# Expert stage of a three-block network: first two activation chunks as one group of 512 columns, and the expert one-hot written by ScalarE from a table

## The chip, the core and the metric

The kernel runs on one core of one Trainium2 chip. The metric is the device time of one execution in microseconds (us), from the first to the last instruction with what lies around them. Engines are named as in the profile: PE is TensorE (PEld its weight loads), DVE is VectorE, ACT is ScalarE, POOL is GpSimd, SP is SyncE, which issues the weight DMAs.

## The reference, cut to what matters

Three network blocks run one after the other on 512 tokens of width 1024. The change touches the mixture of experts at the end of the first block alone:

```python
def moe(h, w_router, b_router, w1, b1, w2, b2):
    """Top-4-of-32 experts with clamped SwiGLU; exact sparse dispatch via expert-sorted blocks."""
...
x = x + gt_f[:, None, :] * moe(h, w_router[l], b_router[l], w_mlp1[l], b_mlp1[l], w_mlp2[l], b_mlp2[l])
```

For each expert, up to 128 of its tokens are gathered. The first product, 1024 to 2048 columns plus bias `b1`, gives a gate half and a linear half. The activation is the gate, clamped above at 7, times its sigmoid (with 1.702), times the clamped linear half plus one. The second product, 1024 to 1024, is scaled by the token's gate and added to the token's row.

## The kernel before

A unit is one expert with up to 128 tokens. There are 34 units in this run (32 experts and spills). The loop body in each engine's program is one unit; the last unit stands behind the loop. All fp32 products are made from pairs of float32r numbers: a high part (`moe_high`, written by ACT, L1802) and a low part (`moe_low`, written by DVE, L1811). A unit has 24 half chunks j of weights (128x1024 each), 16 for the first product and 8 for the second. `high(j)` is one ACT instruction; `low(j)` is one DVE instruction for the halves j and j+1 together (128x2048). Six halves of buffer stand between them and PE, so `high(j)` waits until PE has used half j-6 (semaphore `used`).

`pe_unit` (L2034) sets PE's order. For each of four activation chunks c it adds the bias by a product of the one-hot `moe_esel` with `b1` (L2061), then four `product` calls of six matmuls (L2050 four, L2054 two). The output is bank 0 or 1 of PSUM, by c modulo 2. Behind chunk 1 comes `turn(0)`, two transposes of the activated chunk 0 (L2041); behind chunk 2 `turn(1)`, behind chunk 3 `turn(2)`. Then come the eight halves 16 to 23 of the second product, with the eight transposes of the next unit's tokens (`pe_x_turn`, L2030, into banks 4 and 5) behind half 17, and `turn(3)` behind half 18. A `turn(c)` waits for `multiply(c)` (`act_done`) and for `low_of_turned(c-1)` (`aT`).

`dve_unit` (L1870) sets DVE's order, by hand: between the `low` instructions stand, for each chunk, `clamp` (L1885, linear half out of PSUM), `multiply` (L1891, then L1894, of 256 columns each) and `low_of_turned` (L1879). `dve_stage` (L1845, L1846) writes the next unit's token indices for the gather. It waits for `kept`: POOL's copy L1948 of the present indices, which stands on POOL behind the scatter L1962 of the unit before. `dve_esel` (L1851) writes the one-hot from a PSUM column. `dve_xe_low` (L1858) writes the low part of the next unit's transposed tokens; PE's next unit waits for it (`xe`). `act_unit` (L1979) has the `sigmoid` (L1988), `turned` (L1993, high part of the transposed activations) and `act_xe` (L1976).

Of the kernel before, what the change touches and what calls it, by code (L numbers as in the profile page):

```python
# [20 lines left out]
ALU = mybir.AluOpType  # L21
# [1750 lines left out]
class Experts:  # L1772


    def __init__(self, K, bufs):
        self.K, self.nc, self.B = K, K.nc, bufs
        n_ = lambda s: K.sem(f"moe_{s}")
        self.used, self.high, self.low = n_("used"), n_("high"), n_("low")
        self.picked, self.placed, self.read, self.staged = n_("picked"), n_("placed"), n_("read"), n_("staged")
        self.esel = n_("esel")  # L1780
# [35 lines left out]

    def split(self, part, eng, u, js, ahead):
# [31 lines left out]
    def dve_esel(self, ve, v):  # L1849
        B = self.B  # L1850
        self.nc.vector.tensor_scalar(B["esel"][:, :], B["ps_row"].to_broadcast([P, CAP]),  # L1851
                                     B["unit_f"][:, bass.ds(v, 1)], None, ALU.is_equal).then_inc(self.esel, 1)

    def dve_xe_low(self, ve, v):
        B = self.B
        ve.wait_ge(self.xe_high, v + 1)
        flat = lambda part: B["xe"][:, part, :, :].rearrange("p k n -> p (k n)")
        self.nc.vector.tensor_tensor(flat(1), self.K.ps[:, 4:6, :].rearrange("p a n -> p (a n)"),  # L1858
                                     flat(0).bitcast(F32), ALU.subtract).then_inc(self.xe, 1)
# [10 lines left out]
    def dve_unit(self, ve, u, ahead=True):  # L1870
        nc, B = self.nc, self.B

        def low(*js):
            self.split(self.dve_low, ve, u, js, ahead)

        def low_of_turned(c):
            ve.wait_ge(self.aT_high, u * 4 + (c + 1))
            out = B["aT"][:, :, 2 * c:2 * c + 2, :]
            nc.vector.tensor_tensor(out[:, 1, :, :].rearrange("p a b -> p (a b)"), self.K.ps[:, 3, 0:256],  # L1879
                                    out[:, 0, :, :].rearrange("p a b -> p (a b)").bitcast(F32), ALU.subtract)\  # L1880
                .then_inc(self.aT, 1)

        def clamp(c):
            ve.wait_ge(self.used, u * PER + (4 * c + 4))
            nc.vector.tensor_scalar(B["lin"][:, c % 2, :], self.K.ps[:, c % 2, 256:512], 1.0 + LIMIT, 1.0 - LIMIT,  # L1885
                                    ALU.min, ALU.max).then_inc(self.clamped, 1)

        def multiply(c):
            ve.wait_ge(self.sig, u * 4 + (c + 1))
            ve.wait_ge(self.clamped, u * 8 + (2 * c + 1))  # L1890
            nc.vector.scalar_tensor_tensor(B["glu"][:, c % 2, :], B["sig"][:, c % 2, :], SIG_LIMIT, B["lin"][:, c % 2, :],  # L1891
                                           ALU.min, ALU.mult).then_inc(self.clamped, 1)
            ve.wait_ge(self.clamped, u * 8 + (2 * c + 2))
            nc.vector.scalar_tensor_tensor(B["a"][:, c % 2, :], self.K.ps[:, c % 2, 0:256], LIMIT, B["glu"][:, c % 2, :],  # L1894
                                           ALU.min, ALU.mult).then_inc(self.act_done, 1)
# [78 lines left out]
    def act_xe(self, sc, v):  # L1974
        sc.wait_ge(self.x_turned, v + 1)
        self.nc.scalar.activation(self.B["xe"][:, 0, :, :].rearrange("p k n -> p (k n)"),  # L1976
                                  self.K.ps[:, 4:6, :].rearrange("p a n -> p (a n)"), ACT.Copy).then_inc(self.xe_high, 1)

    def act_unit(self, sc, u, ahead=True):  # L1979
        nc, B = self.nc, self.B  # L1980

        def high(*js):
            self.split(self.act_high, sc, u, js, ahead)

        def sigmoid(c):
            sc.wait_ge(self.clamped, u * 8 + (2 * c + 1))
            sc.wait_ge(self.act_done, u * 4 + (c + 3))
            nc.scalar.activation(B["sig"][:, c % 2, :], self.K.ps[:, c % 2, 0:256], ACT.Sigmoid, scale=ALPHA)\  # L1988
                .then_inc(self.sig, 1)

        def turned(c):
            sc.wait_ge(self.a_turned, u * 4 + (c + 5))
            nc.scalar.activation(B["aT"][:, 0, 2 * c:2 * c + 2, :].rearrange("p a b -> p (a b)"),  # L1993
                                 self.K.ps[:, 3, 0:256], ACT.Copy).then_inc(self.aT_high, 1)
# [32 lines left out]
    def pe_x_turn(self, pe, v):  # L2027
        pe.wait_ge(self.gathered, v * 16 + 16)
        for k in range(KD):
            ins = self.nc.tensor.transpose(self.K.ps[:, 4 + k // 4, (k % 4) * P:(k % 4 + 1) * P],  # L2030
# [3 lines left out]
    def pe_unit(self, pe, u, ahead=True):  # L2034
        nc, ps, B = self.nc, self.K.ps, self.B

        def turn(c):
            pe.wait_ge(self.act_done, u * 4 + (c + 5))
            pe.wait_ge(self.aT, u * 4 + (c + 4))
            for i in range(2):  # L2040
                ins = nc.tensor.transpose(ps[:, 3, i * P:(i + 1) * P], B["a"][:, c % 2, i * P:(i + 1) * P],  # L2041
                                          self.K.ident[:, :])
            ins.then_inc(self.a_turned, 1)
# [15 lines left out]
        for c in range(4):  # L2059
            pe.wait_ge(self.act_done, u * 4 + (c + 3))  # L2060
            nc.tensor.matmul(ps[:, c % 2, :], B["esel"][:, :], B["b1"][:, c * 512:(c + 1) * 512], start=True, stop=False)  # L2061
            for i in range(4):
                product(ps[:, c % 2, :], B["xe"], 4 * c + i, 2 * i, True)
            if c:
                turn(c - 1)
            if c == 0 and ahead:
                self.pe_place(pe, u + 1)
        for j in range(16, 24):
# [3 lines left out]
            if m == 0:  # L2072
                pe.wait_ge(self.aT, u * 4 + (k + 5))
# [3 lines left out]
            if j == 18:  # L2077
                turn(3)
# [7 lines left out]
def mixture(K, posm, gate, gsplit, units, rows, gates_f):  # L2086
# [8 lines left out]
    with ExitStack() as ctx:  # L2095
        sb = lambda name, shape, dt=F32: K.sb(ctx, f"moe_{name}", shape, dt)
        lane = lambda i: K.hT[:, i, :].rearrange("p (b n) -> p b n", b=2)
        iota, from_end, slots = sb("iota", [P, CAP]), sb("from_end", [P, NT]), sb("slots", [P, 8])
# [4 lines left out]
             "ps_row": table[:, 384:385], "ps_place": table[:, 388:392], "from_end": from_end[:, :],  # L2103
# [16 lines left out]
        pair = lambda t: K.ps[:, 6 * ((t + 1) % 2):6 * ((t + 1) % 2) + 2, :]  # L2120
        with nc.Block() as block:
# [41 lines left out]
            def _(ve):  # L2163
# [5 lines left out]
                nc.vector.tensor_copy(B["ps_row"], slots[:, 5:6])  # L2169
# [4 lines left out]
                ve.nop().then_inc(X.act_done, 4)  # L2174
                ve.nop().then_inc(X.aT, 4)
                ve.nop().then_inc(X.y_ready, 2)
                X.dve_esel(ve, 0)
# [36 lines left out]
            def _(sc):  # L2214
# [11 lines left out]
                X.act_xe(sc, 0)  # L2226
                with sc.Fori(0, n1) as u:
# [5 lines left out]
            def _(pe):  # L2233
                n1 = pe.value_load(unit_last[0:1, 0:1], min_val=EXPERTS - 1, max_val=EXPERTS + SPILLS - 1)
                pe.nop().then_inc(X.a_turned, 4)
# [1845 lines left out]
```

## Time and profile before

| | |
|---|---|
| median of 3 runs | 3779.34 us (3778.82 to 3779.49) |
| profiled execution | 3781.95 us |
| its span, first to last instruction | 3780.1 us |
| PE, DVE, ACT, POOL busy, share of the span | 91%, 55%, 46%, 28% |
| the expert loop: first to last scatter of a unit | 875.6 to 2079.1 us, 33 steps |

The busy times are of the whole span; the change lies in the stretch from about 800 to 2080 us, where PE and DVE are both busy nearly all the time. A matmul row's end is modelled, so PE's pace is read from the starts. On DVE and ACT an instruction starts some 0.08 us before the one ahead of it has its end, so there too costs are taken from start to start.

### The profile page before, as it was taken

Reading aid. Unit: us, or ns where it says so; the run is one execution under the profiler, and the core shown is the slowest. Engines: PE = TensorE matmul, PEld = TensorE weight load, DVE = VectorE, ACT = ScalarE, POOL = GpSimd, SP = SyncE. Lnnn points to the kernel's source line nnn. Section 1 sums busy time; section 2 is a strip of 40 time slices with the busy share of each in tenths; the row PEclk is TensorE's granted clock in tenths of the full one; section 3 lists DMA queues with packets and bytes.
Section 4 is the critical chain, followed back from the end, with each engine's and each line's share of the span. In section 5 each row is a group of like instructions: output and inputs, shape, how many; then the busy total and the mean of one; then the engine's idle time right before and its main releaser. Section 6 shows DMA issues by size and latency. Waiting matters only on the chain. (4 is left out here: it accounts for less than half of the span.)

```text
span 3780.1 us, 55651 instructions
## 1 busy us (share of the span) xinstructions
PE 3444.3 (91%) x20889; PEld 2782.7 (74%) x20889; DVE 2088.5 (55%) x2469; ACT 1755.3 (46%) x2286; POOL 1040.9 (28%) x435
## 2 busy tenths in 40 slices
PE   7989999969999999999999687899998886779997
PEld 4877777648888888888887574688877765668876
DVE  2320111259999999999999236411240263246665
ACT  3222333137787777777777325222242342033333
POOL 2334233202322223232231220244432300024443
PEclk9999999969999999999999798799998966789999
DMA  8223433249999999999999327123231200013221
GB/s 270 80 67 95 138 114 123 78 152 366 366 381 370 370 380 365 383 366 375 376 365 374 116 82 267 45 78 100 95 95 56 96 1 5 7 46 101 100 86 43
DMA packets 245432, 696.84 MB, mean 184 GB/s; under 512 B 17846, under 2 KB 149802, under 8 KB 186652
## 3 DMA queue, kind: packets, MB, share of 16 engines
q1 hardware_dynamic: 234956, 657.73, 46.7%
q0 software_dynamic: 9936, 36.18, 3.6%
q8 instruction: 122, 2.00, 0.2%
q10 hardware_dynamic: 384, 0.65, 0.0%
q14 instruction: 34, 0.28, 0.0%
HBM read 668.73 MB, written 30.23 MB: 185 GB/s over the span
## 5 line engine op out<-in xcount | busy, mean ns | idle before, releaser
L311 POOL TENSOR_TENSOR split_w<-ring,split_w 128x1024 fp32r<-128x1024 f32 (+1 forms) x294 | 698.2, 2375 | 1736.7 <-ACT split_w L306 1589.5
L1811 DVE TENSOR_TENSOR moe_low<-ring,moe_high 128x2048 fp32r<-128x2048 f32 x408 | 929.1, 2284 | 23.6 <-ACT moe_high L1802 23.4
L1802 ACT ACTIVATE moe_high<-ring 128x1024 fp32r<-128x1024 f32 x810 | 827.7, 1058 | 103.7 <-PE psum L2054 101.8
L306 ACT ACTIVATE split_w<-ring 128x1024 fp32r<-128x1024 f32 (+1 forms) x294 | 304.7, 1036 | 1034.6 <-PE psum L376 649.2
L2050 PE MATMUL psum<-moe_high,moe_xe 128*128 128x512 f32 x2176 | 586.9, 391 | 0.0
L2050 PEld LDWEIGHTS psum<-moe_high,moe_xe 128*128 128x128 f32 x2176 | 410.4, 189 | 85.2
L1962 POOL DMA_INDIRECT moe_y_rows<-moe_ye,moe_target x34 | 197.4, 5806 | 696.2 <-DVE moe_ye L1866 696.2
L376 PE MATMUL psum<-pair,split_w 128*128 128x512 f32 x1584 | 364.7, 393 | 13.0 <-PEq L128 6.2
L376 PEld LDWEIGHTS psum<-pair,split_w 128*128 128x128 f32 x1584 | 300.5, 190 | 76.5 <-issue 9.1
L376 PE MATMUL psum<-b_pair,split_w 128*128 128x512 f32 x1440 | 334.7, 394 | 12.9 <-PEq L840 7.1
L2054 PE MATMUL psum<-moe_low,moe_xe 128*128 128x512 f32 x1088 | 337.3, 391 | 0.0
L376 PEld LDWEIGHTS psum<-b_pair,split_w 128*128 128x128 f32 x1440 | 272.6, 190 | 72.5 <-issue 16.1
L2050 PE MATMUL psum<-moe_high,moe_aT 128*128 128x512 f32 x1088 | 302.0, 399 | 0.0
L376 PE MATMUL psum<-b_hpair,split_w 128*128 128x512 f32 x1056 | 241.2, 391 | 5.2 <-PEq L579 5.2
L2054 PEld LDWEIGHTS psum<-moe_low,moe_xe 128*128 128x128 f32 x1088 | 204.8, 188 | 43.9
L376 PEld LDWEIGHTS psum<-b_hpair,split_w 128*128 128x128 f32 x1056 | 199.3, 189 | 46.9 <-issue 5.4
L2050 PEld LDWEIGHTS psum<-moe_high,moe_aT 128*128 128x128 f32 x1088 | 196.7, 188 | 35.9
L2054 PE MATMUL psum<-moe_low,moe_aT 128*128 128x512 f32 x544 | 168.3, 391 | 0.0
L362 PE MATMUL psum<-split_w,b_pair 128*128 128x256 f32 x1152 | 144.7, 288 | 4.1 <-PEq L579 2.2
L362 PEld LDWEIGHTS psum<-split_w,b_pair 128*128 128x128 f32 x1152 | 142.1, 196 | 7.3 <-issue 4.5
L528 PE MATMUL psum<-split_w,pair 128*128 128x512 f32 (+1 forms) x720 | 144.0, 361 | 3.3 <-DVE pair L447 1.8
L528 PEld LDWEIGHTS psum<-split_w,pair 128*128 128x128 f32 x720 | 121.9, 189 | 25.5 <-issue 5.2
(589 smaller groups left out, 4336.9 us busy)
## 6 DMA issues: line engine op xcount, KB each, us to landing
ring<-in_w_experts SPq DMA_DIRECT2D x408, 1024.0 KB, 7.5
ring<-in_w_mod SPq DMA_DIRECT2D x48, 1024.0 KB, 7.2
ring<-in_w_in SPq DMA_DIRECT2D x39, 1024.0 KB, 5.3
ring<-in_w_up SPq DMA_DIRECT2D x33, 1024.0 KB, 5.1
ring<-in_w_in SPq DMA_DIRECT2D x44, 512.0 KB, 5.1
ring<-in_w_down SPq DMA_DIRECT2D x20, 1024.0 KB, 5.0
ring<-in_w_gate SPq DMA_DIRECT2D x11, 1024.0 KB, 5.2
ring<-in_w_out SPq DMA_DIRECT2D x8, 1024.0 KB, 6.0
```

The costliest lines, as they stand in the source:

```text
L306: self.nc.scalar.activation(high, raw, ACT.Copy).then_inc(self.K.rounded, 1)
L311: self.nc.gpsimd.tensor_tensor(low, raw, high.bitcast(F32), ALU.subtract).then_inc(self.K.split, 1)
L362: ins = self.nc.tensor.matmul(out, x(a, r0 + k), w[:, b, k, :], start=(opens and r0 + k + a + b == 0), stop=(closes and r0 + k == KD - 1 a ...
L376: ins = self.nc.tensor.matmul(out[:, tile, :], w[:, a, k, cols], pair[:, b, r0 + k, :], start=(r0 + k + a + b == 0), stop=(r0 + k == nk - ...
L528: ins = nc.tensor.matmul(out[:, t, 0:width], x[:, a, k, t * P:(t + 1) * P], w[:, b, k, :], start=(r + k + a + b == 0), stop=(r + k == tota ...
L1802: self.nc.scalar.activation(self.B["high"][:, j % HALVES, :], self.raw(j), ACT.Copy).then_inc(self.high, 1)
L1811: self.nc.vector.tensor_tensor(flat("low"), self.K.ring[:, self.ring_slot(j // 2), :], flat("high").bitcast(F32), ALU.subtract).then_inc(s ...
L1962: self.nc.gpsimd.indirect_dma_start(self.B["y_rows"], bass.IndirectOffsetOnAxis(ap=self.B["target"][:, 0:1], axis=0), self.B["ye"][:, :], ...
L2050: nc.tensor.matmul(out, lhs[:, part, k0 + k, :], high[:, k, :], start=(k0 + k + part == 0 and not started), stop=False)
L2054: ins = nc.tensor.matmul(out, lhs[:, 0, k0 + k, :], low[:, k, :], start=False, stop=(k0 + k == KD - 1))
```

## The change

Chunks 0 and 1 become one group g = 0 of 512 columns, in banks 0 and 1; chunks 2 and 3 are groups 1 and 2 of 256 columns, in banks 4 and 5. `clamp`, `sigmoid`, `multiply`, `turned` and `low_of_turned` run once for a group, three times a unit where it was four. `turn(0)` is four transposes behind chunk 2, `turn(1)` stands behind chunk 3, `turn(2)` behind half 18.
The next unit's tokens are transposed into banks 0 and 1. The one-hot is written by ACT from a table `moe_owns` made once before the loop; DVE's `dve_esel` is gone. `dve_stage` stands where `clamp(0)` and `multiply(0)` no longer come ahead of it.

```diff
+    def banks(self, g):
+        return self.K.ps[:, 0:2, :] if g == 0 else self.K.ps[:, g + 3:g + 4, :]
...
+    def turned_parts(self, g):
+        first, n = (0, 4) if g == 0 else (2 * g + 2, 2)
...
         low(6)
-        clamp(0)
         low(8)
-        multiply(0)
         if ahead:
             self.dve_stage(ve, u + 1)
         low(10)
+        clamp(0)
+        low(12)
+        multiply(0)
+        low(14)
         clamp(1)
-        low(12)
+        low(16)
+        ve.wait_ge(self.a_turned, u * 3 + 4)
         multiply(1)
         low_of_turned(0)
-        low(14)
+        low(18)
         clamp(2)
-        low(16)
+        low(20)
         multiply(2)
         low_of_turned(1)
-        low(18)
-        clamp(3)
-        low(20)
-        multiply(3)
+        low(22)
         low_of_turned(2)
-        low(22)
-        if ahead:
-            self.dve_esel(ve, u + 1)
-        low_of_turned(3)
         low(24)
...
+    def act_esel(self, sc, v):
+        self.nc.scalar.activation(B["esel"][:, :], self.K.ones[:, 0:CAP], ACT.Copy, scale=B["owns"][:, bass.ds(v, 1)])\
+            .then_inc(self.esel, 1)
...
-        high(6, 7, 8, 9)
+        high(6, 7, 8, 9, 10, 11, 12, 13)
         sigmoid(0)
-        high(10, 11, 12, 13)
+        high(14, 15, 16, 17)
         sigmoid(1)
         turned(0)
-        high(14, 15, 16, 17)
+        high(18, 19, 20, 21)
         sigmoid(2)
         turned(1)
-        high(18, 19, 20, 21)
-        sigmoid(3)
+        high(22, 23, 24)
         turned(2)
-        high(22, 23, 24)
-        turned(3)
         if ahead:
             self.act_xe(sc, u + 1)
+            self.act_esel(sc, u + 1)
         high(25, 26, 27, 28, 29)
...
         for c in range(4):
+            out = ps[:, (0, 1, 4, 5)[c], :]
...
-            if c:
-                turn(c - 1)
+            if c >= 2:
+                turn(c - 2)
...
             if j == 18:
-                turn(3)
+                turn(2)
```

Two places of the order matter below. The first is DVE at the beginning of the loop body, from `low(6)` to `dve_stage` and, with the change, on to the first `clamp`. `hT` is the memory of the activations. Before:

```order
L1811 TENSOR_TENSOR moe_low<-ring,moe_high 128x2048 [waits moe_high]
L1884 REGISTER_ALU
L1885 TENSOR_SCALAR hT<-psum 128x256 [waits moe_used]
L1809 REGISTER_ALU
L1811 TENSOR_TENSOR moe_low<-ring,moe_high 128x2048 [waits moe_high]
L1889 ISA
L1890 ISA [waits moe_sig]
L1891 SCALAR_TENSOR_TENSOR hT<-hT 128x256 [waits moe_clamped]
L1893 REGISTER_ALU
L1894 SCALAR_TENSOR_TENSOR hT<-psum,hT 128x256 [waits moe_clamped]
L1842 REGISTER_ALU
L1844 REGISTER_ALU [waits moe_placed]
```

With the change, where `dve_stage` is L1858 and L1859 and the clamp is L1891:

```order
L1811 TENSOR_TENSOR moe_low<-ring,moe_high 128x2048 [waits moe_high]
L1809 REGISTER_ALU
L1811 TENSOR_TENSOR moe_low<-ring,moe_high 128x2048 [waits moe_high]
L1855 REGISTER_ALU
L1857 REGISTER_ALU [waits moe_placed]
L1858 TENSOR_SCALAR moe_source<-psum 128x1 [waits moe_kept]
L1859 ISA
L1859 TENSOR_REDUCE moe_gate_u<-psum 128x1
L1809 REGISTER_ALU
L1811 TENSOR_TENSOR moe_low<-ring,moe_high 128x2048 [waits moe_high]
L1891 TENSOR_SCALAR hT<-psum 128x512 [waits moe_used]
```

The clamp between the two `low` instructions and the multiply behind them have moved below `dve_stage`. The `low(28)` of the pass before stands just ahead of this piece, so three `low` instructions now follow one another.

The second is ACT from `high(24)` to `high(25)`. Before:

```order
L1800 ISA
L1801 ISA
L1802 ACTIVATE moe_high<-ring 128x1024
L1992 REGISTER_ALU
L1993 ACTIVATE moe_aT<-psum 128x256
L1975 REGISTER_ALU
L1976 ACTIVATE moe_xe<-psum 128x1024
L1801 REGISTER_ALU
L1802 ACTIVATE moe_high<-ring 128x1024
```

With the change:

```order
L1802 ACTIVATE moe_high<-ring 128x1024
L1999 REGISTER_ALU
L2001 ACTIVATE moe_aT<-psum 128x256
L1977 REGISTER_ALU
L1978 ACTIVATE moe_xe<-psum 128x1024
L1983 ISA
L1983 ACTIVATE moe_esel<-ones,moe_owns 128x128
L1801 REGISTER_ALU
L1802 ACTIVATE moe_high<-ring 128x1024
```

The one-hot now stands between the copy of the tokens and `high(25)`, for which DVE's `low(24)` waits.

## Rows read from the trace of the kernel before

**Rows 1.** Windows; busy us and count of PE, PEld, DVE, ACT, POOL; clock, DMA share, GB/s
```profile
1200.00:1400.00 200.00, 199.06 (x926) 163.32 (x925) 196.79 (x203) 158.12 (x192) 59.12 (x23) 1.00 0.96 368
```
**Rows 2.** Waits from 850 to 2000 us: total us, times, longest
```profile
PEld psum L2041 <- DVE hT L1894: 19.0, 32, 0.7
...
PE psum L2041 <- DVE moe_aT L1879: 5.2, 23, 0.3
```
**Rows 3.** Timeline of PE, 1240 to 1282 us: start, us, instruction, count, idle before
```profile
1254.98 0.38 PE L2041 MATMUL psum<-identity,hT 128*128 128x128 f32 x2
...
1260.45 0.62 PE L2054 MATMUL psum<-moe_low,moe_xe 128*128 128x512 f32 x2
1260.91 0.38 PE L2041 MATMUL psum<-identity,hT 128*128 128x128 f32 x2
...
1265.68 0.63 PE L2054 MATMUL psum<-moe_low,moe_aT 128*128 128x512 f32 x2
1266.57 0.41 PE L2041 MATMUL psum<-identity,hT 128*128 128x128 f32 x2 [0.26 <-DVE moe_aT L1879]
...
1273.65 0.39 PE L2061 MATMUL psum<-moe_b,moe_esel 128*128 128x512 f32 x1
```
**Rows 4.** Timeline of DVE, 1240 to 1282 us
```profile
1266.01 0.41 DVE L1879 TENSOR_TENSOR moe_aT<-psum,moe_aT 128x256 fp32r<-128x256 f32 x1
...
1268.54 0.35 DVE L1851 TENSOR_SCALAR moe_esel<-psum,unit_f 128x128 fp32r<-128x128 f32 x1
1268.80 0.42 DVE L1879 TENSOR_TENSOR moe_aT<-psum,moe_aT 128x256 fp32r<-128x256 f32 x1
1269.64 2.29 DVE L1811 TENSOR_TENSOR moe_low<-ring,moe_high 128x2048 fp32r<-128x2048 f32 x1 [0.42 <-ACT moe_high L1802]
1271.85 1.22 DVE L1858 TENSOR_TENSOR moe_xe<-psum,moe_xe 128x1024 fp32r<-128x1024 f32 x1
...
1275.18 1.40 DVE L1866 SCALAR_TENSOR_TENSOR moe_ye<-psum,moe_gate_u,b_gates 128x512 f32<-128x512 f32 x2
...
1277.36 4.49 DVE L1811 TENSOR_TENSOR moe_low<-ring,moe_high 128x2048 fp32r<-128x2048 f32 x2
1281.76 0.42 DVE L1885 TENSOR_SCALAR hT<-psum 128x256 f32<-128x256 f32 x1
```
**Rows 5.** Timeline of ACT, 1240 to 1282 us
```profile
1266.35 1.06 ACT L1802 ACTIVATE moe_high<-ring 128x1024 fp32r<-128x1024 f32 x1 [0.66 <-PE psum L2054]
1267.31 0.37 ACT L1993 ACTIVATE moe_aT<-psum 128x256 fp32r<-128x256 f32 x1
1267.58 1.02 ACT L1976 ACTIVATE moe_xe<-psum 128x1024 fp32r<-128x1024 f32 x1
1268.49 1.05 ACT L1802 ACTIVATE moe_high<-ring 128x1024 fp32r<-128x1024 f32 x1
...
1276.27 0.20 ACT L1996 ACTIVATE moe_slots<-ones 128x1 f32<-128x1 f32 x1
1276.38 2.94 ACT L1802 ACTIVATE moe_high<-ring 128x1024 fp32r<-128x1024 f32 x3
```
**Rows 6.** Timeline of DVE, 1280 to 1286 us
```profile
1282.10 2.28 DVE L1811 TENSOR_TENSOR moe_low<-ring,moe_high 128x2048 fp32r<-128x2048 f32 x1
1284.31 0.41 DVE L1891 SCALAR_TENSOR_TENSOR hT<-hT 128x256 f32<-128x256 f32 x1
...
1285.10 0.15 DVE L1845 TENSOR_SCALAR moe_source<-psum 128x1 int32<-128x1 f32 x1
```
**Rows 7.** Timeline of POOL, 1268 to 1290 us
```profile
1277.39 5.93 POOL L1962 DMA_INDIRECT moe_y_rows<-moe_ye,moe_target  x1 [20.40 <-DVE moe_ye L1866]
1282.75 1.68 POOL L1948 COPY moe_rows<-moe_source 128x1 int32<-128x1 int32 x1
1286.16 2.25 POOL L1939 DMA_INDIRECT moe_xg<-moe_h_rows,moe_source  x1 [1.74 <-DVE moe_gate_u L1846]
```
**Rows 8.** Instructions of L1962: duration ns min/median/max, first and last start
```profile
L1962 POOL DMA_INDIRECT moe_y_rows<-moe_ye,moe_target x34: 1577/5934/5938, 875.6 to 2079.1; - x34
```

More of the change, by code:

```diff
@@ L1815, in wait_low, with half @@
         eng.wait_ge(self.low, u * PER + (j + 1))
+    def banks(self, g):
+        return self.K.ps[:, 0:2, :] if g == 0 else self.K.ps[:, g + 3:g + 4, :]
+    def half(self, g, name):
+        return self.B[name][:, 0:2, :] if g == 0 else self.B[name][:, g - 1:g, :]
+    def turned_parts(self, g):
+        first, n = (0, 4) if g == 0 else (2 * g + 2, 2)
+        return lambda part: self.B["aT"][:, part, first:first + n, :].rearrange("p a b -> p (a b)"), n * P
     def split(self, part, eng, u, js, ahead):
@@ L1847, in dve_stage @@
             .then_inc(self.staged, 1)
[L1849 to L1852, printed above, removed]
     def dve_xe_low(self, ve, v):
@@ L1874, in low, with low_of_turned, clamp, multiply @@
             self.split(self.dve_low, ve, u, js, ahead)
[L1876 to L1885, printed above, removed]
+        def low_of_turned(g):
+            ve.wait_ge(self.aT_high, u * 3 + (g + 1))
+            out, n = self.turned_parts(g)
+            nc.vector.tensor_tensor(out(1), self.K.ps[:, 3, 0:n], out(0).bitcast(F32), ALU.subtract).then_inc(self.aT, 1)
+        def clamp(g):
+            ve.wait_ge(self.used, u * PER + (4 * g + 8))
+            nc.vector.tensor_scalar(self.half(g, "lin"), self.banks(g)[:, :, 256:512], 1.0 + LIMIT, 1.0 - LIMIT,
                                     ALU.min, ALU.max).then_inc(self.clamped, 1)
[L1888 to L1891, printed above, removed]
+        def multiply(g):
+            ve.wait_ge(self.sig, u * 3 + (g + 1))
+            ve.wait_ge(self.clamped, u * 6 + (2 * g + 1))
+            nc.vector.scalar_tensor_tensor(self.half(g, "glu"), self.half(g, "sig"), SIG_LIMIT, self.half(g, "lin"),
                                            ALU.min, ALU.mult).then_inc(self.clamped, 1)
-            ve.wait_ge(self.clamped, u * 8 + (2 * c + 2))
-            nc.vector.scalar_tensor_tensor(B["a"][:, c % 2, :], self.K.ps[:, c % 2, 0:256], LIMIT, B["glu"][:, c % 2, :],
+            ve.wait_ge(self.clamped, u * 6 + (2 * g + 2))
+            nc.vector.scalar_tensor_tensor(self.half(g, "a"), self.banks(g)[:, :, 0:256], LIMIT, self.half(g, "glu"),
                                            ALU.min, ALU.mult).then_inc(self.act_done, 1)
         low(6)
-        clamp(0)
         low(8)
-        multiply(0)
         if ahead:
@@ L1983, in high, with sigmoid, turned @@
             self.split(self.act_high, sc, u, js, ahead)
[L1985 to L1988, printed above, removed]
+        def sigmoid(g):
+            sc.wait_ge(self.clamped, u * 6 + (2 * g + 1))
+            sc.wait_ge(self.act_done, u * 3 + (4 if g else 3))
+            nc.scalar.activation(self.half(g, "sig"), self.banks(g)[:, :, 0:256], ACT.Sigmoid, scale=ALPHA)\
                 .then_inc(self.sig, 1)
[L1991 to L1994, printed above, removed]
+        def turned(g):
+            sc.wait_ge(self.a_turned, u * 3 + (g + 4))
+            out, n = self.turned_parts(g)
+            nc.scalar.activation(out(0), self.K.ps[:, 3, 0:n], ACT.Copy).then_inc(self.aT_high, 1)
         nc.scalar.activation(B["unused"], self.K.ones[:, 0:1], ACT.Sigmoid)
-        high(6, 7, 8, 9)
+        high(6, 7, 8, 9, 10, 11, 12, 13)
         sigmoid(0)
-        high(10, 11, 12, 13)
+        high(14, 15, 16, 17)
         sigmoid(1)
         turned(0)
-        high(14, 15, 16, 17)
+        high(18, 19, 20, 21)
         sigmoid(2)
         turned(1)
-        high(18, 19, 20, 21)
-        sigmoid(3)
+        high(22, 23, 24)
         turned(2)
-        high(22, 23, 24)
-        turned(3)
         if ahead:
             self.act_xe(sc, u + 1)
+            self.act_esel(sc, u + 1)
         high(25, 26, 27, 28, 29)
@@ L2035, in pe_unit, with turn @@
         nc, ps, B = self.nc, self.K.ps, self.B
[L2037 to L2042, printed above, removed]
+        def turn(g):
+            pe.wait_ge(self.act_done, u * 3 + (g + 4))
+            pe.wait_ge(self.aT, u * 3 + (g + 3))
+            a = self.half(g, "a").rearrange("p c n -> p (c n)")
+            for i in range(a.shape[-1] // P):
+                ins = nc.tensor.transpose(ps[:, 3, i * P:(i + 1) * P], a[:, i * P:(i + 1) * P], self.K.ident[:, :])
             ins.then_inc(self.a_turned, 1)
@@ L2059, in pe_unit @@
         for c in range(4):
[L2060 to L2061 removed]
+            out = ps[:, (0, 1, 4, 5)[c], :]
+            pe.wait_ge(self.act_done, u * 3 + (1, 1, 2, 3)[c])
+            nc.tensor.matmul(out, B["esel"][:, :], B["b1"][:, c * 512:(c + 1) * 512], start=True, stop=False)
             for i in range(4):
[L2063 to L2065 removed]
+                product(out, B["xe"], 4 * c + i, 2 * i, True)
+            if c >= 2:
+                turn(c - 2)
             if c == 0 and ahead:
```

28 lines of the change are left out of this document (16 added, 12 removed).

## The prediction

> **What bounds the kernel now.** I read the windows first, then the waits, then one unit of the expert loop engine by engine. In the loop both PE (199.06 of 200 us) and DVE (196.79) are busy nearly all the time, at a granted clock of 1.00, the 2.4 GHz level [rows 1]. So neither engine's busy time alone names the bound. The 33 steps from the first to the last scatter take 2079.1 - 875.6 us, that is 36.47 us for a unit [rows 8].
>
> PE waits at one place only, before the transposes L2041 [rows 2]. In the unit of rows 3 two L2054 matmuls take 0.46 us from start to start (1260.45 to 1260.91). The pair at 1265.68, the end of half 18, would let turn(3) start at 1266.14. It starts at 1266.57, after the DVE instruction L1879 that runs 1266.01 to 1266.42 [rows 3, 4]. That is 0.43 us lost in a unit, or 14 us in all; the 24 us of rows 2 count less or more of it, since a matmul's end is modelled. This is all that a better order on DVE can give back.
>
> Why is DVE late there? It also waits at one place: low(24) at 1269.64 waits for high(25) on ACT [rows 4]. From there it runs on without a gap. ACT's chain to it begins at the end of half 18: high(24) at 1266.35, turned(3) 1267.31, the token copy 1267.58, high(25) 1268.49, which ends at 1269.54 [rows 5]. So the bound is a loop through three engines that closes over **two** units:
> - PE's half 18 done (1266.14) to DVE's low(24) (1269.64), through ACT: 3.50 us.
> - DVE from there to the next unit's L1879, and turn(3) on PE at 1266.57 + 36.47 = 1303.04: 33.40 us.
> - PE from that turn to the end of half 18 one unit later: 36.47 - 0.43 = 36.04 us.
>
> The sum is 72.94, twice 36.47. Whatever is saved or added once in a unit in this loop moves the unit by half of it. Without any wait PE's unit would be 36.04.
>
> **The change part by part.** PE does the same products. Eight activation transposes remain eight, in three groups; at most some hundredths are saved. I take 0.
>
> *DVE, fewer and wider instructions.* A 1024-column L1858 has 1.22 us, a 256-column L1879 0.41: 1.05 ns a column [rows 4], so 256 columns are 0.27 us. The 256-column clamp takes 0.34 from start to start (1281.76 to 1282.10) [rows 4, 6], of which 0.07 is fixed. Merging two clamps saves 0.07, merging two low_of_turned 0.07. A multiply pair takes 0.79 (1284.31 to 1285.10) [rows 6]; one wide pair is 0.79 + 2 x 0.27 = 1.33 where two took 1.58, saving 0.25. Together 0.39 less ahead of the last turn. If the wide instructions cost 0.66 each, as the 512-column L1866 (1.40 for two) does [rows 4], four of them cost up to 0.24 more and the saving is 0.15. I take 0.39, since those L1866 also take a scalar per partition, which the merged ones don't.
>
> *DVE, the one-hot gone.* L1851 takes 0.26 (1268.54 to 1268.80) [rows 4], but behind it DVE stands idle until ACT is ready at 1269.64. It is worth nothing.
>
> *ACT, the one-hot added*, on the chain to low(24). Its 128 columns lie between the 1-column row, 0.11 from start to start (1276.27 to 1276.38), and turned, 256 columns, 0.27 [rows 5]. I take 0.15, by the columns; bounds 0.11 and 0.27. It is queued ahead of high(25), low(24) and the low part of the next unit's tokens, for which PE's next unit waits.
>
> *DVE, dve_stage earlier, and a new wait.* It now comes when the third low in a row is through, at 1281.76 + 2.21 = 1283.97 in the time of this unit, instead of 1285.10. It must wait for POOL's copy L1948, which ends at 1282.75 + 1.68 = 1284.43 [rows 7]. That end is 0.05 behind the end of the low that runs 1282.10 to 1284.38 [rows 6]: the copy is held while that low runs. In the new order this low is the third one and ends at 1284.05, the copy then at 1284.10, and stage starts at 1284.14: a wait of 0.17. If the copy didn't move with the low, it would be 1284.43 + 0.04 - 1283.97 = 0.50. I take 0.17. Queued behind it are low(10), the clamps and all turns.
>
> The Trainium skill ("SBUF — State Buffer", "Who interferes with whom") states the rule for the copy: a VectorE instruction with two SBUF inputs keeps a GpSimd instruction that reads SBUF waiting for its whole length. By that rule the wait is 0.17, without it 0.50; the copy's end agrees.
>
> *The other waits.* From low(24) at 1269.64 PE's unit starts 4.01 later (1273.65). In the new order multiply(0) ends, counted through the lows (4.40 for two, 1277.36 to 1281.76) [rows 4] and the pieces above, 20.9 us after low(24), with the wait 21.0; turn(0) could start at 21.2. PE wants it at 1254.98 + 36.47 - 0.24 (the turn that no longer stands behind chunk 1) - 1269.64 = 21.6. It has 0.4 to spare, turn(1) about as much.
>
> The last part of ACT's chain bounds a second thing. L1858 ends at 1273.07 and PE's unit starts at 1273.65 [rows 3, 4]. With 0.15 more on ACT it ends 7.08 after half 18. A start of PE on a fresh release costs 0.15 (L1879's end 1266.42 to 1266.57) to 0.25. So the next unit can't start before 7.23 to 7.33 after half 18, where PE without any wait would be there after 7.51 - 0.43 = 7.08. Even if DVE's lateness vanished, 0.15 to 0.25 of the 0.43 would come back here. **The stall is not removed; it has two more owners in line.**
>
> *The sum.* The loop over two units changes by -0.39 (DVE) + 0.17 (stage) + 0.15 (ACT) = -0.07, so a unit by -0.035. Times 33 this is -1.2 us. The profiled execution took 3781.95 us around a span of 3780.1, so the change gives 3780.8; against the median, which is 2.6 below it, 3778.1. What stands ahead of the loop (one table for one column and one DVE one-hot) is below 0.5.
>
> **The rivals.**
> *A: three lows in a row shut POOL out.* The scatter L1962 takes 5.93 us in the loop and 1.58 at its shortest [rows 8], the shortest being the last, when DVE has ended. It starts at 1277.39, just behind the pair of lows that starts at 1277.36 and holds DVE until 1281.84, and ends 1.48 after them [rows 4, 7]. If it is these two that hold it, and it gets in only where the row of lows ends, the third low holds it 2.21 longer. It then ends at 1283.97 + 1.56 = 1285.53, the copy 0.2 later, and stage waits until 1285.77: 1.80 instead of 0.17. DVE is then late for turn(0) already: 21.2 + 1.6 = 22.8 after low(24), beyond the 21.6 that PE allows. Then a loop over one unit decides: 22.8, PE from turn(0) to the end of half 18 (1254.98 to 1266.14, 11.2, and 0.2 for two more transposes), 3.65 through ACT: 37.85. That is 1.38 more than 36.47, 45.5 us in all: 3825. It begins to be slower than before when stage waits over 0.24, and beyond about 0.8 turn(0) takes over. For it: the numbers fit to 0.02 us. Against it: if single lows let POOL in between them, as the copy gets in between L1811 and L1891 at 1284.4 [rows 6, 7], the scatter should have ended after the first; and its duration is the same to 4 ns between median and longest, as if it ran by its own clock. The same page of the Trainium skill bears on it both ways: the lock is held for one instruction, and descriptor generation is said not to suffer from a tensor_tensor. By it the scatter stays at 5.93, the forecast's case.
>
> *B: DVE's lateness goes and little comes in its place.* No stage wait, ACT's one-hot at 0.11 and a release that costs nothing extra: the loop over two units falls by 0.28, and with PE's transposes some 0.05 more; the unit by 0.17: -5.5 us, 3774. If the wait at PE's unit start is also overstated, the limit is PE alone, 36.04, or -14 us: 3765. For it: DVE has over half a us less work. Against it: the two other owners above.
>
> *C: the new wait is the larger one, 0.50, or the wide instructions cost 0.66.* +0.33 or +0.24 over two units: +0.17 or +0.12 a unit, 3783.5 or 3782. With both, 3787.5.
>
> *D: the order does nothing*, because the turn's wait is only moved from turn(3) to turn(2). This is the forecast itself, to about 1 us.
>
> **How the numbers follow.** A measurement of this kernel can tell about 0.2% (7.6 us) from no change. The forecast with its unknown costs (3772 to 3783) has 0.52, C 0.13, A 0.25, B beyond 3771.8 has 0.07, and something slower that I don't name 0.03. Faster: 0.07, and 0.01 for the forecast's edge, 0.08. Same: 0.52 - 0.01 + 0.12 of C = 0.63, rounded to 0.64. Slower: A, the last of C and the unnamed, 0.28. The forecast's own range is 3772 to 3784; to leave out no more than 2 in 10 the range must take in A: 3771 to 3828.
>
> **What the profile of the changed kernel would show.** Right: a unit of 36.3 to 36.6 us; PE still waiting in front of the transposes behind half 18, by some 0.4 us, for low_of_turned; the scatter still 5.93 us; L1858 (the new stage) 0.1 to 0.2 behind the end of its low; low(24) waiting for high(25) 0.15 later after half 18 than now. Wrong: a scatter near 8 us with a DVE gap of over 1 us in front of stage, and PE waiting at turn(0) (A); a wait at PE's unit start in the place of that at the turn, or none at all (B); the wide multiplies at over 0.7 us from start to start (C).

## The result: slower, by the stall that the first rival priced

| | before | after |
|---|---|---|
| median (4 runs each, same chip) | 3779.08 us | 3842.09 us |
| profiled execution | 3781.95 us | 3836.22 us |
| unit, median of the steps from scatter to scatter | 36.54 us | 38.34 us |
| first to last scatter | 1203.5 us | 1260.9 us |
| scatter's length, median | 5.93 us | 8.14 us |

The ratio is 1.0161, 95% interval 1.0149 to 1.0173. The forecast was 3778.1 with a range of 3771 to 3828: the measured time is 64 us above the one and 14 above the top of the other. By the profiles, the loop is 57.4 us longer, the head before it 2.7; the rest of the difference is no more than what the stretch behind the loop varies by from trace to trace (1691 to 1705 us in all the kernels here). The same spread, some 8 us to either side in a long series of the same kernel, is why the experiments are read by the unit in the trace and not by the median alone.

The windows of the kernel after, 1200 to 1400 us, answer to [rows 1] (PE 199.06, DVE 196.79 there):

```profile
core 0: us, PE busy (x) PEld busy (x) DVE busy (x) ACT busy (x) POOL busy (x), PEclk, DMA share, GB/s
1200.00:1400.00 200.00, 191.57 (x883) 155.09 (x884) 185.88 (x168) 151.18 (x178) 63.70 (x21) 1.00 0.95 358
```

PE and DVE both stand idle now, at the same granted clock of 1.00; the clock has no part in it. The waits of 870 to 2050 us say where (us in total, times, longest):

```profile
DVE moe_source L1858 <- POOL moe_rows L1950: 52.9, 31, 1.7
PE psum L2047 <- DVE hT L1900: 43.5, 31, 1.5
```

Both are new beside [rows 2]: DVE's stage (L1858) waits for POOL's copy (L1950), 1.71 us in each unit, and PE waits at `turn(0)` (L2047) for the wide multiply (L1900). One unit on POOL and on DVE (start, duration, engine, line; idle before in brackets), answering to [rows 7] and [rows 4]:

```profile
1300.02 8.14 POOL L1964 DMA_INDIRECT moe_y_rows<-moe_ye,moe_target  x1 [18.45 <-DVE moe_ye L1874]
1307.58 0.78 POOL L1950 COPY moe_rows<-moe_source 128x1 int32<-128x1 int32 x1
1309.52 2.34 POOL L1941 DMA_INDIRECT moe_xg<-moe_h_rows,moe_source  x1 [1.16 <-DVE moe_gate_u L1859]
```

```profile
1299.99 6.69 DVE L1811 TENSOR_TENSOR moe_low<-ring,moe_high 128x2048 fp32r<-128x2048 f32 x3
1308.39 0.16 DVE L1858 TENSOR_SCALAR moe_source<-psum 128x1 int32<-128x1 f32 x1 [1.71 <-POOL moe_rows L1950]
...
1313.69 0.68 DVE L1897 SCALAR_TENSOR_TENSOR hT<-hT 128x512 f32<-128x512 f32 x1
1314.41 0.69 DVE L1900 SCALAR_TENSOR_TENSOR hT<-psum,hT 128x512 f32<-128x512 f32 x1
...
1330.63 2.29 DVE L1811 TENSOR_TENSOR moe_low<-ring,moe_high 128x2048 fp32r<-128x2048 f32 x1 [1.01 <-ACT moe_high L1802]
```

The three lows end at 1306.68. The scatter ends at 1308.16, 1.48 behind them, just as it ended 1.48 behind two lows before; the copy ends 0.20 later and stage starts 0.03 after that. On PE:

```profile
1315.23 0.65 PE L2047 MATMUL psum<-identity,hT 128*128 128x128 f32 x4 [1.37 <-DVE hT L1900]
...
1326.38 0.63 PE L2059 MATMUL psum<-moe_low,moe_aT 128*128 128x512 f32 x2
1327.23 0.41 PE L2047 MATMUL psum<-identity,hT 128*128 128x128 f32 x2 [0.22 <-DVE moe_aT L1887]
```

The bound is now a loop over one unit. From low(24) (1330.63 - 38.34 = 1292.29) to `turn(0)` it is 22.94, from there to half 18's end (1326.38 + 0.46 = 1326.84) 11.61, from there through ACT to low(24) 3.79: 38.34.

### The profile page after: what moved, and what is told of

It is laid out like the page before. It is cut to its first block and busy times, and to the rows that moved or that the text cites. A ratio compares the mean times of both kernels' runs of the same rounds, so it can differ in the third digit from the quotient of the medians.

```text
span 3834.4 us, 55142 instructions
## 1 busy us (share of the span) xinstructions
PE 3444.9 (90%) x20889; PEld 2773.1 (72%) x20889; DVE 2075.6 (54%) x2299; ACT 1762.0 (46%) x2252; POOL 1102.3 (29%) x435
## 3 DMA queue, kind: packets, MB, share of 16 engines
q0 software_dynamic: 9936, 36.18, 3.6%
## 5 line engine op out<-in xcount | busy, mean ns | idle before, releaser
L1964 POOL DMA_INDIRECT moe_y_rows<-moe_ye,moe_target x34 | 272.3, 8009 | 668.0 <-DVE moe_ye L1874 668.0
```

The lines of the kernel that those rows point to most:

```text
L1964: self.nc.gpsimd.indirect_dma_start(self.B["y_rows"], bass.IndirectOffsetOnAxis(ap=self.B["target"][:, 0:1], axis=0), self.B["ye"][:, :], ...
```

## The experiments

The theory after the result (L): lows, which have two inputs from SBUF, keep the scatter from going on until the row ends when they follow each other with nothing between, 2.20 us for each low; stage then waits for the copy behind it, and everything on DVE behind stage is late. Its rivals: the scatter is longer for a reason of its own (more DMA traffic, the other place in the unit); the wide instructions or the one-hot on ACT make the unit longer, and the wait is only slack that shows at stage.

### Where the row is cut

**e1, e2: a short instruction in the row.** It reads 256 columns of one SBUF tensor and writes one column.

```diff
+    def gap(self):
+        self.nc.vector.tensor_reduce(self.B["spare"], self.K.x[:, 0, 0:256], AX, ALU.add)
...
# e1
         low(6)
+        self.gap()
         low(8)
# e2
+        self.gap()
         low(6)
         low(8)
```

> The changed kernel with one DVE instruction of 256 columns with a single SBUF input (a sum over a row of the residual, its result unused) put between low(6) and low(8); nothing else. Theory L (a row of lows, each with two SBUF inputs, shuts the scatter on POOL out until the row ends): the scatter falls from 8.14 to 5.9 us, dve_stage waits under 0.3 us in place of 1.7, the unit falls from 38.2 to 36.5-36.8 us, the time to 3780-3790. Theory O (the one-hot on ACT and the wide instructions cost the time, the scatter only looks on): the added instruction costs DVE 0.34 us more a unit, the time stays at 3840 or goes up by 5.

> The same added instruction, but between low(28) of the pass before and low(6), so that two lows follow it. Theory L in its plain form (the scatter waits for the first free moment): it starts with low(28), gets in behind it and takes about 3.7 us; stage waits under 0.3 us; time as in the run with the gap between low(6) and low(8), 3780-3790. A form with several accesses that each need a free moment: one in the gap, the rest behind the row, scatter 8 us, time 3840. Theory O: 3840-3845.

e1: unit 37.03, scatter 5.93, 3791.54 us (1.0031 of before, 1.0019 to 1.0044); unit and time are just above the 36.5 to 36.8 and 3780 to 3790 that I expected. e2: unit 36.71, scatter 3.73, 3786.43 us (1.0020, 1.0009 to 1.0031). An instruction that adds 0.33 us to DVE's work takes 1.3 and 1.6 us from each unit. DVE and POOL of e2:

```profile
1316.62 2.29 DVE L1811 TENSOR_TENSOR moe_low<-ring,moe_high 128x2048 fp32r<-128x2048 f32 x1
1318.82 0.42 DVE L1871 TENSOR_REDUCE moe_spare<-x_res 128x1 f32<-128x256 f32 x1
1319.15 4.49 DVE L1811 TENSOR_TENSOR moe_low<-ring,moe_high 128x2048 fp32r<-128x2048 f32 x2
1323.56 0.14 DVE L1858 TENSOR_SCALAR moe_source<-psum 128x1 int32<-128x1 f32 x1
```

```profile
1316.64 3.73 POOL L1969 DMA_INDIRECT moe_y_rows<-moe_ye,moe_target  x1 [24.55 <-DVE moe_ye L1878]
1319.80 1.68 POOL L1955 COPY moe_rows<-moe_source 128x1 int32<-128x1 int32 x1
```

The scatter is let in where the gap is, and runs on while the next low runs. So it is not DVE's load as such that holds it, but what stands ahead of it in a row. The copy behind it got in too, and this L does not explain: it ends at 1321.48, 0.04 behind the first of the two lows (1319.15 + 2.29 = 1321.44), though the second follows it with nothing between. In all units but the last this copy took 1.67 or 1.68.

**e8: the gap with one column.**

```diff
-        self.nc.vector.tensor_reduce(self.B["spare"], self.K.x[:, 0, 0:256], AX, ALU.add)
+        self.nc.vector.tensor_reduce(self.B["spare"], self.K.x[:, 0, 0:1], AX, ALU.add)
```

> The gap between low(6) and low(8) with one column instead of 256: an instruction of about 0.07 us. If the end of the row of two-input instructions is what lets the scatter go on, length doesn't matter: 5.93 us, and the unit 0.2 to 0.3 under that of the long gap, 36.75 to 36.85. If the scatter needs a free stretch of some length, it isn't let in: 8.14 us, a stage wait of 1.7 and a unit of 38.4.

Scatter 5.93, unit 36.75, 3784.81 us (1.0019, 1.0009 to 1.0029). An instruction of 0.06 us from start to start is enough: for the scatter the edge counts, not the length of a free stretch. This is also the changed kernel with next to nothing but the stall removed, so its loop is worth reading: DVE's low(24), PE's `turn(0)`, and the last pair of half 18.

```profile
1312.18 2.29 DVE L1811 TENSOR_TENSOR moe_low<-ring,moe_high 128x2048 fp32r<-128x2048 f32 x1 [1.01 <-ACT moe_high L1802]
```

```profile
1307.95 0.61 PE L2064 MATMUL psum<-moe_low,moe_aT 128*128 128x512 f32 x2
...
1333.56 0.65 PE L2052 MATMUL psum<-identity,hT 128*128 128x128 f32 x4
...
1344.68 0.61 PE L2064 MATMUL psum<-moe_low,moe_aT 128*128 128x512 f32 x2
```

From half 18's end (1307.95 + 0.46 = 1308.41) to low(24) it is 3.77, to `turn(0)` 21.38, to the next half 18's end (1345.14) 11.58, together 36.73.

**e12: one operand out of PSUM.**

```diff
-        low(6)
+        ve.wait_ge(self.high, u * PER + 8)
+        blocks = lambda t: t.rearrange("p (a n) -> p a n", n=P)
+        nc.vector.tensor_tensor(blocks(B["low"][:, 0:2, :].rearrange("p a n -> p (a n)")),
+                                blocks(self.K.ring[:, self.ring_slot(3), :]),
+                                self.K.ps[:, 6, 0:P].unsqueeze(1).to_broadcast([P, 16, P]), ALU.subtract)\
+            .then_inc(self.low, 2)
         low(8)
```

> The changed kernel with the second operand of low(6) read from PSUM (columns of bank 6, 16 times 128) and not from SBUF: the same operation, length and order on DVE, one SBUF input where there were two. The low parts of half 6 are then not the differences that they should be; the work is the same. If what holds the scatter is two inputs from SBUF, it gets in during low(6) and ends 3.73 us after its start, or a little later: 3.7 to 4.4, no stage wait, unit 36.5 to 36.7 by the early gap's. If any long DVE instructions in a row hold it, 8.14 and 38.3.

Its low parts of half 6 are not the right differences, so the kernel serves for its timing alone. Unit 36.50, scatter 3.73, 3778.39 us (0.9996, 0.9987 to 1.0006). The first rows are DVE's, the last two POOL's:

```profile
1277.08 2.28 DVE L1811 TENSOR_TENSOR moe_low<-ring,moe_high 128x2048 fp32r<-128x2048 f32 x1
1279.28 2.28 DVE L1905 TENSOR_TENSOR moe_low<-ring,psum 128x2048 fp32r<-128x2048 f32 x1
1281.48 2.28 DVE L1811 TENSOR_TENSOR moe_low<-ring,moe_high 128x2048 fp32r<-128x2048 f32 x1
1283.68 0.15 DVE L1858 TENSOR_SCALAR moe_source<-psum 128x1 int32<-128x1 f32 x1
```

```profile
1277.10 3.73 POOL L1969 DMA_INDIRECT moe_y_rows<-moe_ye,moe_target  x1 [24.06 <-DVE moe_ye L1874]
1280.26 0.77 POOL L1955 COPY moe_rows<-moe_source 128x1 int32<-128x1 int32 x1
```

DVE is as busy as in the changed kernel, in the same order, for the same 2.28 us an instruction. Only the second SBUF operand of the middle low is gone, and with it 4.4 us of the scatter and the whole stall. Among all the runs this is the one that leaves the least room for another reading.

### The stall and the scatter's length apart

**e7: stage behind the multiply, four lows in a row.**

```diff
         low(8)
-        if ahead:
-            self.dve_stage(ve, u + 1)
         low(10)
         clamp(0)
         low(12)
         multiply(0)
+        if ahead:
+            self.dve_stage(ve, u + 1)
```

> The changed kernel with dve_stage moved behind multiply(0), so that four lows stand in a row (28, 6, 8, 10) and nobody waits early for POOL's copy. If the row of lows holds the scatter, it takes 10.3 us, longer than ever; but since stage no longer waits in front of clamp(0), the unit falls by up to the 1.71 of the stage wait, to 36.6 to 36.9. If the delayed scatter costs time by itself (a later gather, POOL as the bound), the unit stays at 38.3 or is longer. If the scatter ran by its own clock it would be 8.14 again.

Four lows stood in a row in each unit but the last, 2.20 us from start to start. The scatter took 10.34 us in 12 of these 33 units, as expected, but 8.14 in the other 21: there it was let in between the third low and the fourth, with nothing between them. DVE and POOL of one unit of either kind:

```profile
1301.01 8.89 DVE L1811 TENSOR_TENSOR moe_low<-ring,moe_high 128x2048 fp32r<-128x2048 f32 x4
1301.03 10.34 POOL L1964 DMA_INDIRECT moe_y_rows<-moe_ye,moe_target  x1 [20.19 <-DVE moe_ye L1874]
...
1338.85 8.88 DVE L1811 TENSOR_TENSOR moe_low<-ring,moe_high 128x2048 fp32r<-128x2048 f32 x4
1338.86 8.14 POOL L1964 DMA_INDIRECT moe_y_rows<-moe_ye,moe_target  x1 [16.34 <-DVE moe_ye L1874]
```

In DVE's own rows the two kinds look alike. What differs is when low(10), the fourth, has its input ready: ACT's high(11) ended 0.15 to 0.74 us before the start of low(10) in the 12 units, and 0.12 to 0.15 before it in the 21. So a low that becomes ready just ahead of its start seems to let POOL in, and L in its plain form is too simple. No run was made to test this.

Stage never waited. Yet the unit was 38.13 (37.52 to 40.34), 3832.57 us (1.0144, 1.0127 to 1.0161): my expectation of 36.6 to 36.9 was wrong. The time went into another wait. PE now waits for the gathered tokens:

```profile
1323.27 0.61 PE L2059 MATMUL psum<-moe_low,moe_aT 128*128 128x512 f32 x2
1325.01 1.09 PE L2035 MATMUL psum<-identity,moe_xg 128*128 128x128 f32 x8 [1.12 <-DMA moe_xg<-moe_h_rows,moe_source]
```

The gather starts at 1315.01 there instead of 1309.52, and its rows are not there when PE wants to transpose them (42.6 us in 30 waits from 870 to 2050 us). Stage sits between two limits: early, it waits for the scatter; late, PE waits for the gather.

**e15: the kernel before, with the gap.**

```diff
+        self.gap()
         low(6)
         clamp(0)
         low(8)
```

> The kernel before with the one-column gap between low(28) and low(6), nothing else. The scatter falls from 5.93 to 3.73 us. If its length costs nothing where nobody is made to wait, the unit changes by the gap's own 0.07 in the loop over two units, 36.54 to 36.58; if the 5.93 cost something there already, it is below 36.5.

Scatter 3.73, unit 36.56, 3781.36 us (1.0006, 0.9997 to 1.0016). Where nobody waits for it, the scatter's 2.2 us are worth nothing.

### The kernel before, with three lows in a row

**e4, e10, e11.**

```diff
# e4, the kernel before
         low(6)
-        clamp(0)
         low(8)
+        clamp(0)
         multiply(0)
# e10, e4 and
+        self.gap()
         low(6)
         low(8)
# e11, e4 and on ACT
-        high(6, 7, 8, 9)
+        high(6, 7, 8, 9, 10, 11)
         sigmoid(0)
-        high(10, 11, 12, 13)
+        high(12, 13)
```

> The kernel before with one thing changed: low(8) stands ahead of clamp(0), so that low(28), low(6), low(8) follow one another; chunks, widths and one-hot as before. Theory L: the scatter goes from 5.93 to 8.14 us, its copy ends 1.7 us behind the end of low(8), where clamp(0) and multiply(0) take 1.1 us; stage waits 0.6 us. Half of it to all of it goes into the unit: 3790-3800. Theory O: nothing changes but the order, 3779 within 3 us.

e4: scatter 8.14, unit 38.16, 3835.02 us (1.0144, 1.0127 to 1.0161). The scatter did what L says, but the time was far beyond my 3790 to 3800, and stage hardly waited in it. ACT, then DVE:

```profile
1306.60 0.39 ACT L1988 ACTIVATE hT<-psum 128x256 f32<-128x256 f32 x1 [3.86 <-DVE hT L1885]
1306.88 3.90 ACT L1802 ACTIVATE moe_high<-ring 128x1024 fp32r<-128x1024 f32 x4
```

```profile
1306.07 0.42 DVE L1885 TENSOR_SCALAR hT<-psum 128x256 f32<-128x256 f32 x1
1307.13 0.43 DVE L1891 SCALAR_TENSOR_TENSOR hT<-hT 128x256 f32<-128x256 f32 x1 [0.65 <-ACT hT L1988]
...
1308.98 2.34 DVE L1811 TENSOR_TENSOR moe_low<-ring,moe_high 128x2048 fp32r<-128x2048 f32 x1 [0.83 <-ACT moe_high L1802]
```

ACT's `sigmoid(0)` waits 3.86 us for the late clamp and keeps high(10) and high(11) behind it; low(10) then waits for them. So this was perhaps not a witness for L at all. e10 and e11 take the two mechanisms apart.

> The kernel before with low(8) ahead of clamp(0) (three lows in a row, unit 38.16) and the one-column gap between low(28) and low(6). The scatter gets 3.73. If the scatter's length made that kernel slow, the unit falls to 36.5 to 36.8. If it is ACT's queue (sigmoid(0) waits for the late clamp and keeps high(10) and high(11) back), the unit stays at 38.1 to 38.3, since none of this moves.

> The kernel before with low(8) ahead of clamp(0) and, on ACT, high(10) and high(11) ahead of sigmoid(0). Scatter 8.14. If ACT's queue cost the 1.6 us, the wait of low(10) for high(11), 0.83, goes and the unit falls by about that, to 37.2 to 37.5; the rest stays as the wait of multiply(0) for sigmoid(0), 0.65, or of stage for the copy behind the scatter. If the queue has no part in it, 38.1.

e10: scatter 3.73 and unit 38.23 (3837.10 us; 1.0156, 1.0140 to 1.0172): the short scatter changes nothing. e11: scatter 8.14 and unit 37.28 (3802.32 us; 1.0060, 1.0044 to 1.0075): low(10) no longer waits and the unit is shorter by 0.88. So ACT's queue makes a little over half of e4's 1.62. Of the other 0.74 the trace of e11 shows that `multiply(0)` still waits 0.6 us for `sigmoid(0)` in each unit; no run takes this away. That e4 came out near the changed kernel was a coincidence of two different stalls.

### The one-hot, and what is left without the stall

**e3, e5, e6: the one-hot on DVE again, the clamp split.**

```diff
# e3, e6
-            self.act_esel(sc, u + 1)
...
         low(22)
+        if ahead:
+            self.dve_esel(ve, u + 1)
         low_of_turned(2)
# e5, e6
         low(6)
+        clamp_first()
         low(8)
```

> The changed kernel with the one-hot written by DVE again, where the kernel before has it, and not by ACT. The chain from half 18 through ACT to low(24) was 3.79 us in the changed kernel's unit, against 3.50 before. Theory L: the wait of stage at 1.7 us stays, the loop over one unit falls by these 0.29 us: 9 to 10 us less than the changed kernel, about 3832. Theory O: most of the 63 us goes, under 3800.

> The changed kernel with the clamp of its first 512-column group cut in two again: bank 0 is clamped between low(6) and low(8), bank 1 where the wide clamp stood. All operations stay, one more fixed cost on DVE. If the row of lows holds the scatter, the clamp ends the row after two lows as the gap did: scatter 5.93 us, stage waits under 0.2, unit 36.75 to 36.95 (the gap's 37.03 less its own 0.2 to 0.3). If it was something of the gap instruction itself (one SBUF input, written to SBUF) that let the scatter in, a PSUM-reading clamp does not: 8.14 us and 38.4.

> The same, and the expert one-hot on DVE again, in its idle time ahead of low(24), as before the change. If the 0.29 us that the one-hot takes on ACT lies in the loop over one unit, the unit is 0.29 shorter than with the split clamp alone (36.5 to 36.65); if that kernel is bounded by the loop over two units, 0.15 shorter (36.6 to 36.8). With the scatter held by the lows it stays above the 36.54 of before only by what the turns cost; otherwise 38.1.

e3: unit 38.03, 3828.89 us (1.0128, 1.0112 to 1.0145); 0.31 less than with the one-hot on ACT. e5: scatter 5.93, unit 36.75, 3784.36 us (1.0015, 1.0006 to 1.0025). e6: unit 36.52, 3777.25 us (1.0000, 0.9990 to 1.0009); 0.23 less than e5. What it costs on ACT stands in the trace of the kernel after; the next `high` starts 0.29 later:

```profile
1328.27 1.02 ACT L1978 ACTIVATE moe_xe<-psum 128x1024 fp32r<-128x1024 f32 x1
1329.18 0.40 ACT L1983 ACTIVATE moe_esel<-ones,moe_owns 128x128 fp32r<-128x128 f32 x1
1329.47 2.04 ACT L1802 ACTIVATE moe_high<-ring 128x1024 fp32r<-128x1024 f32 x2
```

**e14: the kernel before with this one edit** (`act_esel` behind `act_xe` as in the change, `dve_esel` taken out).

> The kernel before with one edit: the expert one-hot on ACT, from the table, as the change has it. It takes 0.29 from start to start there. In the loop over two units this makes 0.15 a unit, 36.69. If the prediction's 0.15 for one pass held, 36.61. If ACT's lateness decides a loop over one unit here, 36.83. The DVE instruction that goes is worth nothing.

Unit 36.74, where I expected 36.69; 3786.55 us (1.0020, 1.0011 to 1.0030): 0.20 more a unit, 0.41 in the loop over two units. Of this 0.29 is the one-hot (half 18's end to low(24) is 3.79 for 3.50). The other 0.12 lies on PE's side of the loop (36.31 for 36.18), in steps of some hundredths; I did not trace it further.

**e9, e13: one gap and two, both with the one-hot on DVE.**

```diff
# e13 (e9 has the first alone)
+        self.gap(0)
         low(6)
+        self.gap(1)
         low(8)
```

> The changed kernel with a gap of one column between low(28) and low(6), and the one-hot on DVE again. From the 36.71 of the long gap at this place: less 0.13 for the shorter gap (0.27 in the loop over two units), less 0.15 to 0.24 for the one-hot: unit 36.34 to 36.43, 3771 to 3775, faster than the kernel before by 0.1 to 0.2%. Scatter 3.73. Rival: the stall at the turn behind half 18 is set by ACT and PE's unit start, which the changed order doesn't shorten: 36.5, no difference from before.

> The changed kernel with a gap of one column on either side of low(6), and the one-hot on DVE. With one gap stage still waits 0.17 for the copy and costs 0.46 from the end of its low to the next low's start, where it costs 0.14 without a wait. With the second gap the copy gets in ahead of low(8): no wait. The loop over two units is 73.04 in the one-gap kernel; less 0.32, plus 0.07: 72.79, unit 36.40, 4 us less than before in all. Rival: PE's unit start or ACT takes over at once, 36.5.

e9: unit 36.52, 3779.45 us (0.9999, 0.9990 to 1.0008), where I expected 36.34 to 36.43. e13: unit 36.38, 3773.05 us (0.9983, 0.9974 to 0.9992), the one version here that beats both kernels. Around stage, e9 and then e13:

```profile
1314.87 4.49 DVE L1811 TENSOR_TENSOR moe_low<-ring,moe_high 128x2048 fp32r<-128x2048 f32 x2
1319.44 0.16 DVE L1858 TENSOR_SCALAR moe_source<-psum 128x1 int32<-128x1 f32 x1
1319.55 0.16 DVE L1859 TENSOR_REDUCE moe_gate_u<-psum 128x2 f32 x1
1319.73 2.29 DVE L1811 TENSOR_TENSOR moe_low<-ring,moe_high 128x2048 fp32r<-128x2048 f32 x1
```

```profile
1316.63 2.28 DVE L1811 TENSOR_TENSOR moe_low<-ring,moe_high 128x2048 fp32r<-128x2048 f32 x1
1318.83 0.15 DVE L1858 TENSOR_SCALAR moe_source<-psum 128x1 int32<-128x1 f32 x1
1318.90 0.14 DVE L1859 TENSOR_REDUCE moe_gate_u<-psum 128x2 f32 x1
1318.97 2.27 DVE L1811 TENSOR_TENSOR moe_low<-ring,moe_high 128x2048 fp32r<-128x2048 f32 x1
```

In e9 the copy is held by both lows behind the gap, where in e2 it got in between them; around the scatter the two differ in the length of the gap alone, and why that matters stays open. Its row in e9 is 3.61 long, from 1315.79 to 1319.40, and stage starts 0.17 after it could (1314.87 + 4.40 = 1319.27). The two small instructions and the next low then follow 0.11 and 0.18 apart, where they follow 0.07 apart without a wait. Stage thus costs 0.46 and not 0.14. In e13 the copy gets in at the second gap and the 0.32 are saved for a gap of 0.06; the DVE part of the loop falls from 33.38 to 33.11.

## Why the prediction was wrong, step by step

**The bound and the method held.** Both loops were the right ones. In e9 the loop over two units is 3.48 + 33.38 + 36.18 = 73.04, twice 36.52. The unit of 36.47 in the prediction was a mean that the shorter last step pulls down; the median is 36.54, and the wait at the turn is 0.36 in the median unit, not 0.43. So PE's own part of the loop is 36.18, not 36.04.

**DVE's wider instructions held** to 0.01: the wide multiply pair takes 1.33 (1313.69 to 1315.02 in the kernel after), clamp and low_of_turned 0.60 each. The 0.39 were really saved.

**The step that failed is "dve_stage earlier, and a new wait".** It put the copy's end 0.05 behind the third low and took 0.17. That needed the scatter to keep its 5.93 us. What the runs showed in its place: the third low holds it 2.20 longer, 8.14 us, and stage starts 1.80 late. The argument for 5.93 was that single lows let POOL in between them, as the copy gets in at 1284.4 [rows 6, 7], and that a duration the same to 4 ns is a clock of its own. The second reading was wrong: the duration is so even because DVE's row is. It is 3.73, 5.93 and 8.14 us behind one, two and three lows, and 10.34 in 12 of 33 units behind four, each time 2.20 or 2.21 more. The first reading carried over to the scatter what the copy did ahead of a multiply of 256 columns. POOL can indeed get in between two lows (the copy of e2, the scatter in 21 units of e7), but the scatter never did so between the first three. Why not is open. A low of 2.28 us starts 2.20 after the one ahead, 0.08 before that one's end, so that no moment is without a low; but this is so in the 21 units of e7 as well, so it is not enough as a cause. What is shown is that one instruction between two lows (of one column from SBUF, or a clamp out of PSUM), or a PSUM operand in one of them, lets the scatter in each time.

**Rival A was right in its mechanism and nearly in size.** It gave 22.8, 11.4 and 3.65, that is 37.85; the kernel after has 22.94, 11.61 and 3.79. These 0.49 us, times 33, are the 16 by which its 3825 fell short, and with it the top of the range; 0.14 of them is the one-hot. The stage wait was 1.80 with its start-up, as it said. Its chance of 0.25 was too low: "the numbers fit to 0.02 us" was evidence from the trace, and what stood against it was an analogy.

**The one-hot on ACT was mis-sized.** 0.15 with bounds of 0.11 and 0.27 was worked out from columns; it is 0.29, outside the bounds. It is shorter than `turned` by half the columns and yet dearer; what makes it so, the scale read per partition or the table's place, was not separated. With it alone the kernel before is 0.2% slower (e14).

**`turn(0)` had no 0.4 to spare.** In e8, without the stall, the loop through `turn(0)` is already the longest, 36.73; by the prediction's own pieces it would have been 3.65 + 21.2 + 11.4 = 36.25. The step compared `turn(0)` with the low(24) of the kernel before, and left out that ACT's longer chain moves low(24) towards `turn(0)`; and a short stage wait costs 0.32 more than no wait, not 0.17. So without rival A the change would have been near 36.75 a unit or 3784 us, as in e5 and e8, some 0.1 to 0.2% slower, rather than 36.44.

**Rival B** (faster) could not come: both of its conditions, no stage wait and a one-hot of 0.11, were off. e12, which has no stage wait, is still at 36.50 with the one-hot on ACT. **Rival C**'s 0.66 for a wide instruction did not show in the sum: the first multiply of the pair is 0.72 from start to start (1313.69 to 1314.41), but the pair is the 1.33 of the forecast.

**The Trainium skill** ("SBUF — State Buffer", "Who interferes with whom") says that a VectorE instruction with two SBUF inputs contends with a GpSimd instruction that reads SBUF, and that one with a single SBUF input doesn't. The runs agree: e12's PSUM operand lets the scatter in, whose index column lies in SBUF. The page's "Summary: rules for kernel authors" has the GpSimd instruction blocked until the VectorE instruction finishes; here the scatter was held over up to four of them. The section also infers that descriptor generation is spared by `tensor_tensor`. The forecast named this for its 5.93. Here an indirect DMA that takes 1.58 us on an idle DVE takes up to 10.34, whichever part of it is held: its reading of the index column or its descriptor generation. The runs don't tell these apart.

## What to carry to other kernels

Where the duration of a GpSimd instruction matches a row of VectorE instructions to some hundredths, suspect that the row holds it, and test it with an instruction put between. Then count what the change does to the row, not to the instruction. When an order brings two-SBUF-input instructions together, look at who waits for POOL, and put something that reads PSUM or one operand between them; a column was enough here. And compute each wait anew with all terms of the change in it: slack taken from the kernel before is gone if another term of the same change moves its other end.

## What the runs showed of the hardware

- The scatter by indirect DMA took 1.58 us with DVE idle, and 3.73, 5.93, 8.14 us behind one to three lows of 2.20 us in a row. Behind four it took 10.34 in 12 units and 8.14 in 21 (e7). Once let in, it ran on under the next low (e2, e8, e9).
- An instruction of one column and one SBUF input (0.06 us from start to start) between two of them let POOL in (e8, e9, e13); so did a clamp out of PSUM (e5) and a PSUM operand in one of them (e12).
- A POOL copy of one column took 0.78 us behind the scatter in the kernel after, and 3.61 when it was held by two lows in a row (e9); in e2 it got in between two such lows and took 1.68.
- Small DVE instructions after a short wait cost more than the wait: three starts that lie 0.07 apart (e13) lie 0.11 and 0.18 apart behind a wait of 0.17 (e9).
- An ACT instruction of 128 columns with a scale from SBUF took 0.29 us from start to start, more than a PSUM copy of 256 columns (0.27).
